# Third up product in wide multiplications over bank pairs, with GpSimd multiplying by the norm row

## The chip, the cores and the metric

The kernel runs on one core of a Trainium2 chip. Its time is the device time of one execution in microseconds (us); the number given for a kernel is the median over several runs. Beside it there is one profiled execution, from which all rows below come. The core has five engines that run side by side and wait for each other through semaphores: TensorE (PE, its weight loads PEld), VectorE (DVE), ScalarE (ACT), GpSimd (POOL) and SyncE (SP), which starts the transfers. TensorE writes to PSUM, which has 8 banks of 512 float32 for each of 128 partitions; all else lies in SBUF.

## The reference

Two blocks of a transformer run over one sequence of T = 256 tokens with 1024 features, all in float32. The first block has a short-convolution layer and a dilated-attention layer, each with a SwiGLU. The second ("hybrid") block has a gated mixture of attention and pooling, and then this feed-forward part, to which the change belongs:

```python
def causal_depthwise_conv(u, w, b):     # kernel width 3: token t sees t, t-1, t-2
def rmsnorm(x, g):
    y = xf * lax.rsqrt(jnp.mean(xf * xf, axis=-1, keepdims=True) + EPS)
    return (y * g).astype(x.dtype)
...
    h2 = rmsnorm(x, norm_ffn_g)
    up = causal_depthwise_conv(h2 @ w_up, conv_w, conv_b)
    gate, val = jnp.split(up, 2, axis=-1)
    return x + (jax.nn.silu(gate) * val) @ w_down
```

w_up is 1024 x 5632, w_down 2816 x 1024. The factor 1/rms of a token can be taken out of the product: h2 @ w_up is (x g) @ w_up, times one number per token, the "norm row".

## The kernel before

Float32 accuracy is made out of three products in a reduced format: each operand is split into a high part and a low rest, and high x high, high x low and low x high are summed in PSUM. ScalarE makes the high part of the weights (`w_hi`, line 1359) and VectorE the low rest (`w_lo = raw - w_hi`, line 1858). Activations are kept the same way, in `x_both`, where for each k the 256 tokens of `x_hi` stand beside the 256 of `x_lo` only by a stride, so that one multiplication of 512 columns can read both.

All weights stream through in chunks. A chunk of the third up product (`up2`, 22 chunks, written j = 0 to 3 within turns i, of which i = 1 to 4 are a hardware loop) is 1024 x 256: 8 blocks of k by 2 blocks of 128 output features. Even j is a gate chunk, odd j the value chunk for the same features; a unit is one pair. A chunk passes through these hands:

- SyncE loads it in two halves (line 583) into one of two raw buffers once VectorE is through with the raw chunk two before (`lo_ready`).
- ScalarE splits off the high part three chunks ahead of the one that it is treating, VectorE the low part two chunks ahead (`ahead(..., split, 3)` and `ahead(..., split, 2)`). Both are 2 instructions of 128x1024. There are four weight slots.
- TensorE waits for `lo_ready` and for the bank (`ready`), then runs `feature_major` (lines 667 to 686): for each of the 2 blocks and 8 k three multiplications of 256 columns, all into one bank, `s = (ph.n0 + j) % 4`. For `up2` this is bank 3, 0, 1, 2 for j = 0 to 3.
- VectorE multiplies the bank by the norm row (`rstd`, read again for both blocks through a stride of zero, `by_token`) into `scaled` (line 2053), and signals `emptied`. Then it does its weight splits.
- ScalarE makes the tap of the token itself with the bias, `gate = scaled * w2 + b` (line 1550, two instructions), and signals `conv_base`. For an even chunk it then makes the high part of the unit before (`last_high`, line 1538), for an odd one the silu of the gate (line 1558), and after that its weight split.
- VectorE adds the two earlier tokens (line 2063, four instructions of 128x255 or 128x254) and signals `taps_done`.
- GpSimd multiplies silu(gate) by value for a unit (`mid`, line 2497) and, when ScalarE has its high part, subtracts to get the low one (`a_lo`, line 2488). It does nothing else in this phase.

The first two chunks are treated apart (line 1169): their multiplications are interleaved with the last turning of x, and the norm row is only made in their course, through bank 7. After `up2` comes `down2`, 8 chunks of 5 or 6 k by 512 columns, whose first weights are split while the last up chunks are treated: these splits are of 128x1536 (or 1024).

The first block's up products (`up0`, `up1`) already use `gated_blocks` (lines 826 to 839). There the high weights are multiplied by both halves of `x_both` in one multiplication of 512 columns into a whole bank per block (left half high x high, right half high x low), and the low weights by `x_hi` in one of 256 into the left half. ScalarE copies the right halves out of the two banks, VectorE adds the left halves to them, and VectorE multiplies by the norm row.

Of the kernel before, what the change touches and what calls it, by code (L numbers as in the profile page):

```python
# [32 lines left out]
T = 256  # L33
# [64 lines left out]
def build(nc, a, out):  # L98
# [4 lines left out]
    with ctx:  # L103
# [218 lines left out]
        silu_done = sem("silu_done")  # L322
        conv_base = sem("conv_base")
        taps_done = sem("taps_done")
        gates_set = sem("gates_set")
        mid_ready = sem("mid_ready")
        mid_hi = sem("mid_hi")
# [88 lines left out]
        ROW_BANK = {0: 6, 1: 3, 2: 7, 3: 3, 4: 7, 5: 7}  # L416
        first_unit = {"up0": 0, "up1": 1}
        UNIT_TURN = 2
        NORM_OF = {"up0": 1, "up1": 3}

        def made(ph, u):
# [237 lines left out]
        def _(pe):  # L659
# [460 lines left out]
            def emit(ph):  # L1120
# [46 lines left out]
                elif name == "up2":  # L1167
                    def body(j, i):
                        if isinstance(i, int) and i == 0 and j < 2:
                            if j == 1:  # L1170
                                return
                            ready(ph, 0, 0)
                            feature_part(ph, 0, x_hi, x_lo, 5, 0, 3)
                            turn_x_pairs(5, 1)
                            feature_part(ph, 0, x_hi, x_lo, 5, 3, 4)
                            ready(ph, 1, 0)
                            feature_part(ph, 1, x_hi, x_lo, 5, 0, 4)
                            feature_part(ph, 0, x_hi, x_lo, 5, 4, KD).then_inc(product_done, 1)
                            row(5)
                            feature_part(ph, 1, x_hi, x_lo, 5, 4, KD).then_inc(product_done, 1)  # L1180
                            return
                        ready(ph, j, i)
                        feature_major(ph, j, x_hi, x_lo)
                    run(pe, ph, body, peel=1)
                elif name in ("pool_in", "gates_a"):
                    if name == "pool_in":
# [162 lines left out]
        def _(act):  # L1349
# [190 lines left out]
            def up_conv_body(ph):  # L1540

                def body(j, i):
                    first = isinstance(i, int) and i + j == 0
                    u = i * 2 + j // 2
                    if j % 2 == 0 and not first:
                        act.wait_ge(mid_ready, 4 + u)
                    wait_emptied(act, ph, j, i)
                    for m in range(2):
                        f = i * 4 + (j // 2 * 2 + j % 2 * KF + m)
                        ins = nc.scalar.activation(gate[:, j % 2, m, :], scaled[:, j % 2, m, :], ACT.Identity,  # L1550
                                                   bias=vec[:, ds(f + col["conv_b_2"], 1)],
                                                   scale=vec[:, ds(f + col["conv_w_2_2"], 1)])
                    ins.then_inc(conv_base, 1)
                    if j % 2 == 0 and not first:
                        last_high(ph, u - 1)
                    if j % 2 == 1:
                        act.wait_ge(taps_done, i * 4 + j)
                        nc.scalar.activation(flat2(gate[:, 0]), flat2(gate[:, 0]), ACT.Silu).then_inc(silu_done, 1)
                    ahead(ph, j, i, split, 3)
                return body  # L1560

            def softmax_exp(src, spans, c, at_):
# [283 lines left out]
        def _(dve):  # L1846
# [198 lines left out]
            def up_conv_body(ph):  # L2045

                def body(j, i):
                    first = isinstance(i, int) and i == 0 and j < 2
                    s = (ph.n0 + j) % 4
                    dve.wait_ge(product_done, ph.n(j, i) + 1)  # L2050
                    if not first:
                        dve.wait_ge(taps_done, i * 4 + (j - 1))
                    nc.vector.tensor_tensor(scaled[:, j % 2], ps[:, s, :].rearrange("p (m t) -> p m t", m=2),
                                            by_token(rstd), ALU.mult).then_inc(emptied[s], 1)
                    if not (first and j == 0):
                        ahead(ph, j, i, split, 2)
                    dve.wait_ge(conv_base, i * 4 + (j + 1))
                    wait_emptied(dve, ph, j, i)
                    for back in (1, 2):
                        for m in range(2):  # L2060
                            f = i * 4 + (j // 2 * 2 + j % 2 * KF + m + (2 - back) * 2 * KF)
                            o = gate[:, j % 2, m, back:T]
                            ins = nc.vector.scalar_tensor_tensor(
                                out=o, in0=scaled[:, j % 2, m, 0:T - back],
                                scalar=vec[:, ds(f + col["conv_w_2_01"], 1)], in1=o, op0=ALU.mult, op1=ALU.add)
                        if back == 1:
                            link(ins)
                    ins.then_inc(taps_done, 1)
                return body
# [411 lines left out]
        def _(pool):  # L2481
# [6 lines left out]
                nc.gpsimd.tensor_tensor(lo[:, ds(k0, 2), :], mid[:, half], hi[:, ds(k0, 2), :], ALU.subtract)\  # L2488
                    .then_inc(mid_split, 1)

            def last_unit(i, half):

                u = i * 2 + half
                pool.wait_ge(silu_done, u + 1)
                pool.wait_ge(taps_done, u * 2 + 2)
                pool.wait_ge(mid_split, u + unit0["up2"])
                nc.gpsimd.tensor_tensor(flat2(mid[:, 0]), flat2(gate[:, 0]), flat2(gate[:, 1]), ALU.mult)\
                    .then_inc(mid_ready, 1)
                hidden_low(a_hi, a_lo, u + unit0["up2"], u * 2, 0)

            def pool_windows():

# [12 lines left out]
            for ph, bi in order():  # L2515
                if ph is not None:
# [2 lines left out]
                        for i in range(4):  # L2519
                            hidden_low(a_hi, a_lo, i, 2 * i, i % 2)  # L2520
                    elif name == "up2":
                        last_unit(0, 0)
                        last_unit(0, 1)
                        with pool.Fori(1, 5) as i:
                            for half in range(2):
                                last_unit(i, half)
                        last_unit(5, 0)
                    elif name == "branches":
                        for j in range(4):
                            pool.wait_ge(mid_hi, unit0[name] + j + 1)  # L2530
                            nc.gpsimd.tensor_tensor(mix_lo[j // 2][:, j % 2 * 2:j % 2 * 2 + 2, :], mid[:, j % 2],
                                                    mix_hi[:, 2 * j:2 * j + 2, :], ALU.subtract).then_inc(mid_split, 1)
                    elif name == "pool_in":
                        pool.wait_ge(product_done, by_name["qkv2a"].n0)
                        nc.gpsimd.memset(u_pad[:, :, 0:16], 0.0).then_inc(zeroed, 1)
                        pool.wait_ge(hybrid_in, 5 * 16)
                        for l in range(2):
                            wait_emptied(pool, ph, l, 0)
                        pool_windows()
# [66 lines left out]
```

## Time and profile before

| | |
|---|---|
| median of 3 runs | 1084.68 us (1083.58 to 1085.16) |
| the profiled execution | 1083.43 us, its span 1081.4 us |
| PE busy | 1070.7 us, 99% |
| DVE busy | 804.5 us, 74% |
| ACT busy | 647.8 us, 60% |
| POOL busy | 54.5 us, 5% |
| granted TensorE clock | 1.00 |

Busy times are unions of instructions' spans on an engine. The timeline gives an instruction's start and its length; on TensorE, which is pipelined, the distance from one start to the next says what an instruction costs, not its length. VectorE's and ScalarE's instructions overlap their neighbours by some 0.1 us, so there, too, distances from start to start are the better measure of a sequence. An instruction's length includes the time in which it stands still after it has started.

### The profile page before, as it was taken

What the parts mean: (1) busy time and instruction counts of PE and PEld (TensorE: products, weight loads), DVE (VectorE), ACT (ScalarE), POOL (GpSimd) and SP (SyncE); (2) the same over time, 40 slices, a digit from 0 to 9 for tenths busy, and PEclk for the clock granted to TensorE, in tenths of its full rate; (3) what the DMA queues carried; (4) which work ended last, traced back from release to release, by engine and by line L of the source; (5) the groups of instructions that cost most, each with busy time, mean ns of one, the idle gap of its engine ahead of it and who ended that gap; (6) DMA issues with size and microseconds to landing.
All of it is one profiled execution on the core that took longest, in us unless ns stands there. A gap on an engine that the chain in (4) does not pass through costs nothing.

```text
span 1081.4 us, 19548 instructions
## 1 busy us (share of the span) xinstructions
PE 1070.7 (99%) x7436; PEld 970.6 (90%) x7436; DVE 804.5 (74%) x1217; ACT 647.8 (60%) x976; POOL 54.5 (5%) x47
## 2 busy tenths in 40 slices
PE   8999999999999999999999999999999999999998
PEld 8998888888899999888878888889999989999987
DVE  5976878775598778788578778636796778889960
ACT  6546746464588777777576465535465756556650
POOL 0100000000000000000000000000200111222300
PEclk9999999999999999999999999999999999999999
DMA  8555665777286766652256657753454664665660
GB/s 273 174 192 180 210 213 163 239 256 223 78 226 188 200 172 171 184 164 86 82 176 218 208 174 250 274 157 98 136 166 132 200 214 121 191 192 177 235 234 20
DMA packets 220557, 195.91 MB, mean 181 GB/s; under 512 B 10137, under 2 KB 196045, under 8 KB 220493
## 3 DMA queue, kind: packets, MB, share of 16 engines
q1 hardware_dynamic: 220137, 194.82, 57.8%
q8 instruction: 43, 0.70, 0.3%
q10 hardware_dynamic: 356, 0.22, 0.1%
q14 instruction: 21, 0.17, 0.0%
HBM read 191.85 MB, written 1.05 MB: 178 GB/s over the span
## 4 chain that ended last, share of the span: by engine, by line
PE 91%; DVE 3%; ACT 2%; SPq 1%; DMA 1%; issue 1%; DVEq 0%; ACTq 0%
PE ps L833 14%; PE ps L682 8%; PE ps L683 8%; PE ps L684 8%; PE ps L837 7%; PE ps L739 7%; PE ps L738 7%; PE ps L737 7%; PE ps L906 6%; PE ps L907 3%; PE ps L852 2%; PE ps L851 2%; PE ps L850 2%; DVE w_lo L1858 2%; ACT w_hi L1359 1%; PE ps L751 1%
## 5 line engine op out<-in xcount | busy, mean ns | idle before, releaser
L1858 DVE TENSOR_TENSOR w_lo<-raw,w_hi 128x1024 fp32r<-128x1024 f32 (+1 forms) x298 | 399.0, 1382 | 56.4 <-ACT w_hi L1359 55.5
L1359 ACT ACTIVATE w_hi<-raw 128x1024 fp32r<-128x1024 f32 (+1 forms) x298 | 331.3, 1156 | 119.1 <-PE ps L739 38.2
L682 PE MATMUL ps<-x_both,w_hi 128*128 128x256 f32 x656 | 186.8, 285 | 0.2 <-DVE w_lo L1858 0.2
L684 PE MATMUL ps<-x_both,w_lo 128*128 128x256 f32 x656 | 185.6, 283 | 0.0
L683 PE MATMUL ps<-x_both,w_hi 128*128 128x256 f32 x656 | 185.6, 283 | 0.0
L833 PE MATMUL ps<-x_both,w_hi 128*128 128x512 f32 x640 | 153.0, 391 | 0.0
L833 PEld LDWEIGHTS ps<-x_both,w_hi 128*128 128x128 f32 x640 | 117.6, 188 | 23.4 <-DVE w_lo L1858 0.7
L682 PEld LDWEIGHTS ps<-x_both,w_hi 128*128 128x128 f32 x656 | 125.8, 192 | 1.8 <-issue 1.3
L683 PEld LDWEIGHTS ps<-x_both,w_hi 128*128 128x128 f32 x656 | 125.9, 192 | 0.0
L684 PEld LDWEIGHTS ps<-x_both,w_lo 128*128 128x128 f32 x656 | 125.8, 192 | 0.0
L737 PE MATMUL ps<-w_hi,a_hi 128*128 128x512 f32 x296 | 115.7, 391 | 0.0
L738 PE MATMUL ps<-w_lo,a_hi 128*128 128x512 f32 x296 | 115.2, 389 | 0.0
L739 PE MATMUL ps<-w_hi,a_lo 128*128 128x512 f32 x296 | 115.2, 389 | 0.0
L837 PEld LDWEIGHTS ps<-x_both,w_lo 128*128 128x128 f32 x640 | 82.1, 191 | 3.1
L837 PE MATMUL ps<-x_both,w_lo 128*128 128x256 f32 x640 | 83.0, 283 | 0.0
L739 PEld LDWEIGHTS ps<-w_hi,a_lo 128*128 128x128 f32 x296 | 55.6, 188 | 11.6
L738 PEld LDWEIGHTS ps<-w_lo,a_hi 128*128 128x128 f32 x296 | 55.6, 188 | 11.2
L737 PEld LDWEIGHTS ps<-w_hi,a_hi 128*128 128x128 f32 x296 | 55.6, 188 | 11.2
L1496 ACT ACTIVATE gu<-ps 128x512 f32<-128x512 f32 x20 | 12.0, 599 | 88.5 <-PE ps L837 88.5
L1597 ACT ACTIVATE rot_x<-rot_s 32x512 f32<-32x512 f32 x84 | 52.9, 630 | 15.9 <-DVE rot_s L2114 15.1
L906 PE MATMUL ps<-m_both,w_hi 128*128 128x512 f32 x168 | 60.4, 402 | 0.3 <-DVE v_tok L2153 0.3
L906 PE MATMUL ps<-x_both,w_hi 128*128 128x512 f32 x168 | 60.1, 399 | 0.0
(260 smaller groups left out, 1793.2 us busy)
## 6 DMA issues: line engine op xcount, KB each, us to landing
raw<-in_ffn_w_gate_up SPq DMA_DIRECT2D x80, 512.0 KB, 5.3
raw<-in_w_up SPq DMA_DIRECT2D x44, 512.0 KB, 4.4
raw<-in_ffn_w_down SPq DMA_DIRECT2D x24, 768.0 KB, 6.3
raw<-in_conv_w_in SPq DMA_DIRECT2D x24, 512.0 KB, 5.0
raw<-in_w_q SPq DMA_DIRECT2D x48, 256.0 KB, 4.7
raw<-in_w_kv SPq DMA_DIRECT2D x48, 256.0 KB, 4.4
raw_v<-in_w_kv SPq DMA_DIRECT2D x48, 256.0 KB, 3.8
raw<-in_w_in SPq DMA_DIRECT2D x20, 512.0 KB, 4.7
```

Source lines behind the costliest of these rows:

```text
L682: nc.tensor.matmul(o, wh[:, k0 + k, c], hi[:, k, :], start=(k == 0), stop=False)
L683: nc.tensor.matmul(o, wh[:, k0 + k, c], low, start=False, stop=False)
L684: ins = nc.tensor.matmul(o, wl[:, k0 + k, c], hi[:, k, :], start=False, stop=(k == kt - 1))
L737: nc.tensor.matmul(o, high, wh[:, k, :], start=(first and k == ks[0]), **flags)
L738: nc.tensor.matmul(o, high, wl[:, k, :], start=False, **flags)
L739: ins = nc.tensor.matmul(o, low, wh[:, k, :], start=False, **flags)
L833: nc.tensor.matmul(o, wh[:, k, c], x_both[:, :, (k) * T:(k + 1) * T], start=(k == 0), stop=False, skip_group_check=True)
L837: ins = nc.tensor.matmul(o[:, 0, :], wl[:, k, c], x_hi[:, k, :], start=False, stop=(k == KD - 1), skip_group_check=True)
L906: nc.tensor.matmul(o, wh[:, k, c], x, start=(k == 0), stop=False, skip_group_check=True)
L1359: nc.scalar.activation(w_hi[:, s, a * ph.cols:b * ph.cols], src, ACT.Copy)\
L1597: ins = nc.scalar.activation(rot_x[f:f + 32, :, :], rot_s[o:o + 32, n, :, :], ACT.Copy)
L1858: nc.vector.tensor_tensor(w_lo[:, s, c], src, w_hi[:, s, c], ALU.subtract)\
```

## The change

From the third chunk of `up2` on, TensorE uses `gated_blocks` over the bank pair `CONV_BANK[j]` = 2, 0, 4, 6 for j = 0 to 3, with its one product_done per chunk. In front of the fourth chunk (i, j) = (0, 3), TensorE waits until VectorE has emptied the first. ScalarE, at the head of each such chunk, waits for the product and for the taps of two chunks before, copies the right halves of the pair to `scaled`, and does its weight split right behind the copy, no longer at the end. VectorE adds the left halves to the copy and signals `emptied`. GpSimd then multiplies `scaled` by the norm row in place and signals `conv_scaled`, for which ScalarE's and VectorE's tap instructions wait. GpSimd's earlier work is interleaved with it: product of the unit before, multiplication for the even chunk, low part of the unit before, multiplication for the odd chunk.

```diff
+        CONV_BANK = (2, 0, 4, 6)
...
                         ready(ph, j, i)
-                        feature_major(ph, j, x_hi, x_lo)
+                        if isinstance(i, int) and (i, j) == (0, 3):
+                            wait_emptied(pe, ph, 0, 0)
+                        gated_blocks(ph, j, (0, 1), CONV_BANK[j], 0).then_inc(product_done, 1)
...
+                    plain_ = isinstance(i, int) and i == 0 and j < 2
+                    if not plain_:
+                        act.wait_ge(product_done, ph.n(j, i) + 1)
+                        act.wait_ge(taps_done, i * 4 + (j - 1))
+                        nc.scalar.activation(scaled[:, j % 2], ps[:, CONV_BANK[j]:CONV_BANK[j] + 2, T:2 * T], ACT.Copy)\
+                            .then_inc(conv_low, 1)
+                        ahead(ph, j, i, split, 3)
                     if j % 2 == 0 and not first:
                         act.wait_ge(mid_ready, 4 + u)
-                    wait_emptied(act, ph, j, i)
+                    if plain_:
+                        wait_emptied(act, ph, j, i)
+                    else:
+                        act.wait_ge(conv_scaled, i * 4 + (j - 1))
...
-                    ahead(ph, j, i, split, 3)
+                    if plain_:
+                        ahead(ph, j, i, split, 3)
...
-                    dve.wait_ge(product_done, ph.n(j, i) + 1)
-                    if not first:
-                        dve.wait_ge(taps_done, i * 4 + (j - 1))
-                    nc.vector.tensor_tensor(scaled[:, j % 2], ps[:, s, :].rearrange("p (m t) -> p m t", m=2),
-                                            by_token(rstd), ALU.mult).then_inc(emptied[s], 1)
+                    if first:
+                        ...
+                    else:
+                        dve.wait_ge(conv_low, i * 4 + (j - 1))
+                        nc.vector.tensor_tensor(scaled[:, j % 2], ps[:, CONV_BANK[j]:CONV_BANK[j] + 2, 0:T], scaled[:, j % 2],
+                                                ALU.add).then_inc(emptied[s], 1)
                     if not (first and j == 0):
                         ahead(ph, j, i, split, 2)
                     dve.wait_ge(conv_base, i * 4 + (j + 1))
-                    wait_emptied(dve, ph, j, i)
+                    if first:
+                        wait_emptied(dve, ph, j, i)
+                    else:
+                        dve.wait_ge(conv_scaled, i * 4 + (j - 1))
...
+            def scale_chunk(i, j):
+
+                wait_emptied(pool, by_name["up2"], j, i)
+                nc.gpsimd.tensor_tensor(scaled[:, j % 2], scaled[:, j % 2], by_token(rstd), ALU.mult).then_inc(conv_scaled, 1)
...
+            def conv_unit(i, half):
+
+                u = i * 2 + half
+                last_product(u - 1)
+                scale_chunk(i, 2 * half)
+                last_low(u - 1)
+                scale_chunk(i, 2 * half + 1)
```

## Rows read from the trace of the kernel before

**Rows 1.** The page: busy us (share) and instructions; the chain by engine.
```profile
PE 1070.7 (99%) x7436; PEld 970.6 (90%) x7436; DVE 804.5 (74%) x1217; ACT 647.8 (60%) x976; POOL 54.5 (5%) x47
...
PE 91%; DVE 3%; ACT 2%; SPq 1%; DMA 1%; issue 1%; DVEq 0%; ACTq 0%
```

**Rows 2.** Windows: stretch, busy us of PE, PEld, DVE, ACT, POOL, clock, DMA.
```profile
5.00:10.00 5.00, 2.68 (x17) 1.98 (x17) 1.86 (x5) 2.46 (x5) 0.00 (x0) 1.00 1.00 337
904.00:1019.00 115.00, 115.00 (x958) 114.91 (x957) 104.23 (x141) 74.22 (x102) 28.47 (x20) 1.00 0.61 192
```

**Rows 3.** Timeline of PE, third up product's and down product's start: start us, us, what.
```profile
903.17 0.28 PE L682 MATMUL ps<-x_both,w_hi 128*128 128x256 f32 x1
...
1018.37 0.40 PE L737 MATMUL ps<-w_hi,a_hi 128*128 128x512 f32 x1
...
1018.60 0.40 PE L738 MATMUL ps<-w_lo,a_hi 128*128 128x512 f32 x1
```

**Rows 4.** Timeline of PE, the first block's first up product.
```profile
115.70 3.93 PE L833 MATMUL ps<-x_both,w_hi 128*128 128x512 f32 x16
119.46 2.08 PE L837 MATMUL ps<-x_both,w_lo 128*128 128x256 f32 x16
121.37 0.60 PE L823 MATMUL ps<-ident,mid_t 128*128 128x128 f32 x4
...
228.03 0.40 PE L737 MATMUL ps<-w_hi,a_hi 128*128 128x512 f32 x1
```

**Rows 5.** Timeline of DVE, one pair of chunks in the loop.
```profile
937.93 0.69 DVE L2053 TENSOR_TENSOR scaled<-ps,rstd 128x512 f32<-128x512 f32 x1
938.53 2.35 DVE L1858 TENSOR_TENSOR w_lo<-raw,w_hi 128x1024 fp32r<-128x1024 f32 x2
940.80 1.90 DVE L2063 SCALAR_TENSOR_TENSOR gate<-scaled,vec,gate 128x255 f32<-128x255 f32 x4
943.78 0.69 DVE L2053 TENSOR_TENSOR scaled<-ps,rstd 128x512 f32<-128x512 f32 x1 [1.08 <-PE ps L684]
946.65 2.94 DVE L2063 SCALAR_TENSOR_TENSOR gate<-scaled,vec,gate 128x255 f32<-128x255 f32 x4
```

**Rows 6.** Timeline of ACT: the same pair, and a copy in the first block.
```profile
938.79 1.10 ACT L1550 ACTIVATE gate<-scaled,vec 128x256 f32<-128x256 f32 x2 [2.19 <-DVE scaled L2053]
...
944.71 1.10 ACT L1550 ACTIVATE gate<-scaled,vec 128x256 f32<-128x256 f32 x2 [2.39 <-DVE scaled L2053]
945.71 0.61 ACT L1538 ACTIVATE a_hi<-mid 128x512 f32 x1
946.23 2.00 ACT L1359 ACTIVATE w_hi<-raw 128x1024 fp32r<-128x1024 f32 x2
...
172.65 0.60 ACT L1496 ACTIVATE gu<-ps 128x512 f32<-128x512 f32 x1 [5.06 <-PE ps L837]
```

**Rows 7.** Timeline of POOL: a unit in the loop, and a subtraction of the branches.
```profile
942.78 1.29 POOL L2497 TENSOR_TENSOR mid<-gate 128x512 f32<-128x512 f32 x1 [6.49 <-DVE gate L2063]
946.52 1.38 POOL L2488 TENSOR_TENSOR a_lo<-mid,a_hi 128x512 f32 x1 [2.45 <-ACT a_hi L1538]
...
856.03 1.55 POOL L2531 TENSOR_TENSOR mix_lo<-mid,mix_hi 128x512 fp32r<-128x512 f32 x1 [63.05 <-ACT mix_hi L1817]
```

**Rows 8.** Timelines of DVE and POOL where they meet; two undisturbed ones (945.52, 1024.74).
```profile
945.52 1.22 DVE L1858 TENSOR_TENSOR w_lo<-raw,w_hi 128x1024 fp32r<-128x1024 f32 x1
946.65 1.52 DVE L2063 SCALAR_TENSOR_TENSOR gate<-scaled,vec,gate 128x255 f32<-128x255 f32 x1
...
909.74 1.96 DVE L1858 TENSOR_TENSOR w_lo<-raw,w_hi 128x1024 fp32r<-128x1024 f32 x1
...
1015.40 2.59 POOL L2488 TENSOR_TENSOR a_lo<-mid,a_hi 128x512 f32 x1 [2.32 <-ACT a_hi L1538]
...
1024.74 0.48 DVE L2063 SCALAR_TENSOR_TENSOR gate<-scaled,vec,gate 128x254 f32<-128x254 f32 x1
...
1025.14 1.75 DVE L1858 TENSOR_TENSOR w_lo<-raw,w_hi 128x1536 fp32r<-128x1536 f32 x1
...
1026.80 2.32 DVE L1858 TENSOR_TENSOR w_lo<-raw,w_hi 128x1024 fp32r<-128x1024 f32 x1
...
1025.35 2.69 POOL L2497 TENSOR_TENSOR mid<-gate 128x512 f32<-128x512 f32 x1 [7.36 <-DVE gate L2063]
```

**Rows 9.** Timelines of DVE and POOL at the third chunk.
```profile
909.13 0.69 DVE L2053 TENSOR_TENSOR scaled<-ps,rstd 128x512 f32<-128x512 f32 x1
909.74 3.09 DVE L1858 TENSOR_TENSOR w_lo<-raw,w_hi 128x1024 fp32r<-128x1024 f32 x2
912.75 2.82 DVE L2063 SCALAR_TENSOR_TENSOR gate<-scaled,vec,gate 128x255 f32<-128x255 f32 x4
...
909.31 1.29 POOL L2497 TENSOR_TENSOR mid<-gate 128x512 f32<-128x512 f32 x1 [35.83 <-DVE gate L2063]
```

**Rows 10.** Timeline of ACT: the weight splits behind the second chunk.
```profile
908.18 2.00 ACT L1359 ACTIVATE w_hi<-raw 128x1024 fp32r<-128x1024 f32 x2
```

More of the change, by code:

```diff
@@ L324, in build @@
         taps_done = sem("taps_done")
+        conv_low, conv_scaled = sem("conv_low"), sem("conv_scaled")
         gates_set = sem("gates_set")
@@ L2049, in body @@
                     s = (ph.n0 + j) % 4
-                    dve.wait_ge(product_done, ph.n(j, i) + 1)
-                    if not first:
-                        dve.wait_ge(taps_done, i * 4 + (j - 1))
-                    nc.vector.tensor_tensor(scaled[:, j % 2], ps[:, s, :].rearrange("p (m t) -> p m t", m=2),
-                                            by_token(rstd), ALU.mult).then_inc(emptied[s], 1)
+                    if first:
+                        dve.wait_ge(product_done, ph.n(j, i) + 1)
+                        nc.vector.tensor_tensor(scaled[:, j % 2], ps[:, s, :].rearrange("p (m t) -> p m t", m=2),
+                                                by_token(rstd), ALU.mult).then_inc(emptied[s], 1)
+                    else:
+                        dve.wait_ge(conv_low, i * 4 + (j - 1))
+                        nc.vector.tensor_tensor(scaled[:, j % 2], ps[:, CONV_BANK[j]:CONV_BANK[j] + 2, 0:T], scaled[:, j % 2],
+                                                ALU.add).then_inc(emptied[s], 1)
                     if not (first and j == 0):
@@ L2489, in hidden_low, with last_product @@
                     .then_inc(mid_split, 1)
-            def last_unit(i, half):
-                u = i * 2 + half
+            def scale_chunk(i, j):
+                wait_emptied(pool, by_name["up2"], j, i)
+                nc.gpsimd.tensor_tensor(scaled[:, j % 2], scaled[:, j % 2], by_token(rstd), ALU.mult).then_inc(conv_scaled, 1)
+            def last_product(u):
                 pool.wait_ge(silu_done, u + 1)
@@ L2498, in last_unit, with last_low @@
                     .then_inc(mid_ready, 1)
+            def last_low(u):
                 hidden_low(a_hi, a_lo, u + unit0["up2"], u * 2, 0)
+            def conv_unit(i, half):
[4 more added lines that the diff above has]
+                scale_chunk(i, 2 * half + 1)
             def pool_windows():
@@ L2521, in _ @@
                     elif name == "up2":
-                        last_unit(0, 0)
-                        last_unit(0, 1)
+                        conv_unit(0, 1)
                         with pool.Fori(1, 5) as i:
                             for half in range(2):
-                                last_unit(i, half)
-                        last_unit(5, 0)
+                                conv_unit(i, half)
+                        conv_unit(5, 0)
+                        last_product(10)
+                        last_low(10)
                     elif name == "branches":
```

## Prediction

> **What bounds the kernel now.** I read the page first: the busy table, then the chain that ended last. TensorE is busy 99% of the span and 91% of the chain is its matmuls [rows 1], so a change pays only through TensorE's own time, and costs only if it makes TensorE wait. Next the windows of the stage that the diff touches (third chunk to last of the hybrid up product, about 904 to 1019 us): TensorE is busy all of 115.0 us, but VectorE is at 104.2 us, ScalarE 74.2, GpSimd 28.5 [rows 2]. VectorE has 9% spare there: it is the next bound. So I read its timeline in that stage [rows 5] together with GpSimd's [rows 7], because two engines that look far from full can still block each other.
>
> **TensorE's part.** Removed: 16 x 3 = 48 multiplications of 256 columns per chunk. The stage runs from 903.17 us to the first down matmul at 1018.37: 115.20 us for 20 chunks, 5.76 a chunk, 120 ns a matmul [rows 3]. Added: 16 of 512 and 16 of 256 columns, which is what the first block's up product already does: from 115.70 to 228.03 us, less 0.81 us from 121.37 to 122.18 for two other jobs of TensorE, is 111.52 us for 20 chunks, 5.58 a chunk [rows 4]. The merge saves 0.184 us a chunk, 3.7 us in all. Its bounds are these two rows; nothing else in TensorE's stream changes, and the new bank pairs give as many chunks of room as the old banks (four). The added wait of the fourth chunk is for a VectorE instruction that began at 900.95 us, some 7 us before that chunk starts; it is over, and costs nothing.
> By the Trainium skill ("TensorE: Matmul & The Clock Gate", section Back-to-back issue gap) a warm matmul costs its columns plus about 2.5 ns; merging two would then save 16 x 2.5 ns a chunk, an estimate of 0.8 us in all. The rows above show 120 ns for 256 columns and about 228 for 512 (3.76 us from 115.70 to 119.46 for 16, the first included), so the trace gives more to the merge than the page does.
>
> **What the chain behind it gains.** Per chunk before: VectorE's scale out of PSUM (0.69 us, next instruction 0.60 later), two weight splits (2.27 us from start to next start), four tap instructions (1.75, about 0.1 more inside the loop for register work), 4.7 in all; ScalarE: two gates 1.10, two splits 2.0, silu or high copy 0.62 [rows 5, 6]. The change adds a ScalarE copy of 128x512 out of PSUM (0.60, the same copy stands in the first block [rows 6]), swaps VectorE's scale for an add of the same shape (one operand in PSUM; I take 0.69), and adds a GpSimd multiplication of 128x512 per chunk, 20 of them. GpSimd's only like operation takes 1.29 us, its subtraction 1.38 [rows 7]. ScalarE gets to about 4.3 us a chunk and GpSimd to 2 x 1.29 + 1.29 + 1.38 = 5.3 a pair: both fit in 11.15. On the shares alone, the change is free.
>
> **What those shares hide.** Where a GpSimd operation overlaps a VectorE instruction whose two inputs are both in SBUF, one of them stands still. Three places show VectorE held [rows 8]: a tap takes 1.52 instead of 0.48 us when GpSimd's subtraction starts 0.13 us ahead of it (+1.04); the split of 1024 columns takes 1.96 instead of 1.22 when the product is in its last part (+0.74) and 2.32 when GpSimd was waiting (+1.10). GpSimd in turn takes 2.59 us (at 1015.40) and 2.69 (at 1025.35, in the split of 1.75 that began at 1025.14): it waits for that one instruction, goes in between, and holds the next. VectorE's scale, with one input in PSUM, is not held: 0.69 beside GpSimd's 1.29 [rows 9]. A price of 1.05 to 1.10 per meeting, then. GpSimd's new multiplication begins on the very signal after which VectorE starts its two splits, so all 20 meet.
> The Trainium skill ("SBUF — State Buffer", section Who interferes with whom) has this as a lock that is held for the whole instruction, the loser fully blocked, also for a VectorE instruction with two SBUF inputs. The trace agrees in kind, and shows 1.05 rather than the whole 1.29 to 1.39 as lost; by the page's whole duration 40 new or kept meetings would cost an estimated 9 us more than my sum.
>
> **The walk, pair of chunks by pair of chunks, when VectorE sets the pace.** Times from the start of VectorE's add.
> Even chunk: the add 0.61. GpSimd's product of the unit before runs until 1.47 (909.31 + 1.29 - 909.13), so the splits take 3.01 (909.74 to 912.75) [rows 9]. Meanwhile GpSimd's new multiplication waits; it gets in after the first split at 2.5, ends at about 3.7, and holds the second split 1.08: splits over at 0.61 + 3.01 + 1.08 = 4.7. ScalarE's gates run 3.7 to 4.85, taps start at 4.9, take 1.75, and meet GpSimd's subtraction (+1.05), as they do in the loop now. 7.7, with register work 7.85.
> Odd chunk: 0.61 + 2.27 + 1.08 = 3.96 for add and splits; multiplication over at 1.75 + 1.2 = 2.95, gates at 4.1, taps 4.15 to 5.9; 6.05 with register work.
> A pair: 13.9 us, 6.95 a chunk, against 11.52 now and 11.15 that TensorE would want. TensorE gets the weights of chunk n + 2 only from the splits of chunk n, so it falls to this pace.
>
> **The sum.** Chunk 2's slot begins later than now: ScalarE does its copy only after the splits that run 908.18 to 910.17 [rows 10], so the add starts at about 910.8 instead of 909.13; this slot is free of the product and takes 6.9. Chunk 3: 5.95, to 923.7. Eight pairs (chunks 4 to 19): 111.2, to 1034.9. In chunk 20 the splits are those of the down weights, 1.75 instead of 1.22 each, so they end at 1034.9 + 4.7 + 1.06 = 1040.7, and that is when the down product can start; now it starts at 1018.37. +22.3 us. Chunk 21's splits end at about 1048.7, as the first down chunk ends (8.2 us, 36 matmuls of 0.23 [rows 3]); from there VectorE has little to do per down chunk and catches up, so nothing more is lost and nothing given back. The slack that swallows the first losses (now a chunk's weights are ready some 2.9 us ahead: splits over 2.87 us after the add's start, 943.78 to 946.65 [rows 5], against 5.76) is in this, because I compare ends, not paces. The profiled execution took 1083.43 us with a span of 1081.4; 1083.43 + 22.3 = 1105.7. It lay 1.25 below the median of the runs, so I name 1106.
>
> **Bounds.** Below: no waiting of VectorE for gates at all, the pair 13.4 instead of 13.9: -5 us. If a multiplication with the broadcast norm row holds VectorE only as the product's last part did (0.74): 20 x 0.34 = -7 more. Above: broadcast operand as dear as GpSimd's slowest like operation (1.55 [rows 7]): +0.26 on hold and gates, +5; a hand-off of 0.2 us instead of the near zero I took at two places a chunk (ScalarE's gates start 0.17 to 0.24 after the scale [rows 5, 6]): +6. Its own range: 1094 to 1119.
>
> **Rivals.**
> A, faster: the new multiplication holds nothing, or only idle time. Then the chain after a product is copy 0.6, add 0.7, multiplication 1.3, gates 1.1, taps 1.86 = 5.6 plus hand-offs, next add due at 5.58 + 0.65: it fits, TensorE keeps its pace and 3.7 us are won: 1083.4 - 3.7 = 1079.7. For it: shares; GpSimd's product sits mostly in VectorE's idle time today. Against: that idle time is after the taps, and the new multiplication doesn't fall there. 8%.
> B, slower still: VectorE's two splits go back to back and GpSimd gets in only behind them. Odd chunk: multiplication 2.9 to 4.1, gates to 5.3, taps to 7.2; even chunk 9.0; a pair 16.3: 8 x 2.4 + 3 = 22 more, 1128. Against it: GpSimd's 2.69 us at 1025.35 ended before the second split did [rows 8]. 7%.
> C, in between: only a part of the meetings cost (VectorE at 12.0 to 12.6 a pair, so 8 x 1.9 to 8 x 1.3 us below the forecast, a little less in the first chunks): 1089 to 1095. For it: I know no case in which GpSimd reads a broadcast row. 9%.
> D: TensorE's gaps of 1.4 in 7 us drop its granted clock to the 1.2 GHz level; matmuls at twice the time are 11 us a chunk, over 1180. Against: with 2.68 of 5 us busy, at 5 to 10 us, the clock column says 1.00 [rows 2]. 2%.
>
> **How the numbers follow.** Forecast 74%, C 9, A 8, B 7, D 2. The range 1089 to 1128 holds the forecast's own, C, and B at its edge; what is left out is A, D and the tails. A difference under 0.2% (2.2 us) can't be told from none by such runs: faster 8%, within 1%, slower 91%.
>
> **What would show it.** In the windows of the stage: TensorE busy well below the stretch, VectorE near full. The weight splits' mean on VectorE from 1.24 to about 1.9 us; the new GpSimd line at about 2 us, with its wait inside; a chunk at 6.9 to 7.0 us by VectorE's adds; TensorE idle before the 512-column line, released by VectorE's weight split. Wrong if the splits stay at 1.22 us, or if chunks come at 5.58.

## The result and the profile after

The changed kernel takes 1107.88 us (median of 4 runs, 1106.04 to 1110.7), the kernel before 1084.92 us (4 runs): ratio 1.0212, 95% interval 1.0194 to 1.0230. Forecast were 1106 us and a slower kernel. The profiled execution took 1106.04 us with a span of 1104.3.

The page first: busy times by engine, and the chain that ended last, by engine.

```profile
PE 1071.6 (97%) x7116; PEld 954.6 (86%) x7116; DVE 830.7 (75%) x1217; ACT 662.0 (60%) x996; POOL 98.7 (9%) x67
...
PE 79%; DVE 7%; ACT 4%; POOL 4%; issue 3%; DMA 1%; SPq 1%; ACTq 0%; DVEq 0%; POOLq 0%
```

TensorE's busy time is nearly as before [rows 1]: 320 matmuls fewer, but as many columns. What tells is that its idle time in the span grew from 10.7 to 32.7 us, that its share of the chain fell from 91 to 79%, and that GpSimd is now in the chain with 4%. The window of the stage says the same; columns as in [rows 2].

```profile
904.00:1019.00 115.00, 97.56 (x539) 83.32 (x538) 106.66 (x116) 71.90 (x103) 57.48 (x32) 1.00 0.49 149
```

In the same 115 us TensorE is busy 97.6 us instead of 115.0, and VectorE 106.7 instead of 104.2. The stage itself, from TensorE's timeline: first wide matmul, one start in the middle, first down matmul.

```profile
902.66 3.82 PE L835 MATMUL ps<-x_both,w_hi 128*128 128x512 f32 x16
...
934.90 3.92 PE L835 MATMUL ps<-x_both,w_hi 128*128 128x512 f32 x16 [1.28 <-DVE w_lo L1873]
...
1041.13 0.50 PE L739 MATMUL ps<-w_hi,a_hi 128*128 128x512 f32 x1 [2.15 <-DVE w_lo L1873]
```

From 902.66 to 1041.13 us are 138.5, against 115.2 [rows 3]: +23.3, the whole of the loss (the medians differ by 23.0). In nearly every chunk TensorE waits for VectorE's weight split before the first 512-column matmul, 18 times and 19.9 us in all. One pair of chunks on VectorE, to be compared with [rows 5]:

```profile
922.87 0.68 DVE L2071 TENSOR_TENSOR scaled<-ps,scaled 128x512 f32<-128x512 f32 x1
923.47 4.26 DVE L1873 TENSOR_TENSOR w_lo<-raw,w_hi 128x1024 fp32r<-128x1024 f32 x2
928.17 2.72 DVE L2084 SCALAR_TENSOR_TENSOR gate<-scaled,vec,gate 128x255 f32<-128x255 f32 x4 [0.43 <-ACT gate L1564]
930.81 0.68 DVE L2071 TENSOR_TENSOR scaled<-ps,scaled 128x512 f32<-128x512 f32 x1
931.41 3.44 DVE L1873 TENSOR_TENSOR w_lo<-raw,w_hi 128x1024 fp32r<-128x1024 f32 x2
935.18 1.91 DVE L2084 SCALAR_TENSOR_TENSOR gate<-scaled,vec,gate 128x255 f32<-128x255 f32 x4 [0.33 <-ACT gate L1564]
937.00 0.68 DVE L2071 TENSOR_TENSOR scaled<-ps,scaled 128x512 f32<-128x512 f32 x1
```

The even chunk takes 7.94 us (922.87 to 930.81), the odd one 6.19, a pair 14.13 instead of 11.5. Two splits take 3.44 instead of 2.35 where GpSimd's new multiplication meets them, 4.26 where its product does too. GpSimd's side of it, to be compared with [rows 7] and [rows 9]:

```profile
923.13 1.29 POOL L2522 TENSOR_TENSOR mid<-gate 128x512 f32<-128x512 f32 x1 [3.13 <-DVE gate L2084]
924.38 2.28 POOL L2515 TENSOR_TENSOR scaled<-scaled,rstd 128x512 f32<-128x512 f32 x1
928.73 1.49 POOL L2509 TENSOR_TENSOR a_lo<-mid,a_hi 128x512 f32 x1 [2.07 <-ACT a_hi L1542]
931.57 2.20 POOL L2515 TENSOR_TENSOR scaled<-scaled,rstd 128x512 f32<-128x512 f32 x1 [1.35 <-DVE scaled L2071]
```

The multiplication stands behind VectorE's first split and then holds the second. All this is the forecast's walk. One thing on ScalarE's timeline is not: its weight split behind the copy waits for a transfer, 2.67 us here and 2.94 at the most, and the gates stand behind it.

```profile
935.47 0.58 ACT L1553 ACTIVATE scaled<-ps 128x512 f32<-128x512 f32 x1
936.42 1.06 ACT L1363 ACTIVATE w_hi<-raw 128x1024 fp32r<-128x1024 f32 x1 [0.37 <-DMA raw<-in_w_up]
940.15 1.06 ACT L1363 ACTIVATE w_hi<-raw 128x1024 fp32r<-128x1024 f32 x1 [2.67 <-DMA raw<-in_w_up]
941.12 1.08 ACT L1564 ACTIVATE gate<-scaled,vec 128x256 f32<-128x256 f32 x2
```

In the kernel before that split stood last in the chunk, and ScalarE waited for transfers of `w_up` nowhere in this stage. In 14 of the 20 chunks the gates then still wait for GpSimd's product, 18.3 us in all; in the others, as above, the late split is what they waited for. So a total as forecast is no proof of its parts. The experiments take the parts away one at a time.

### The profile page after: what moved, and what is told of

The parts are those of the page before. It is cut to its first block, busy times and chain, and to the rows that moved or that the text cites. A ratio compares the mean times of both kernels' runs of the same rounds, so it can differ in the third digit from the quotient of the medians.

```text
span 1104.3 us, 18956 instructions
## 1 busy us (share of the span) xinstructions
PE 1071.6 (97%) x7116; PEld 954.6 (86%) x7116; DVE 830.7 (75%) x1217; ACT 662.0 (60%) x996; POOL 98.7 (9%) x67
## 3 DMA queue, kind: packets, MB, share of 16 engines
HBM read 191.85 MB, written 1.05 MB: 175 GB/s over the span
## 4 chain that ended last, share of the span: by engine, by line
PE 79%; DVE 7%; ACT 4%; POOL 4%; issue 3%; DMA 1%; SPq 1%; ACTq 0%; DVEq 0%; POOLq 0%
PE ps L835 14%; PE ps L839 7%; PE ps L739 7%; PE ps L741 7%; PE ps L740 7%; PE ps L908 6%; PE ps L684 4%; PE ps L685 4%; PE ps L686 4%; DVE w_lo L1873 3%; PE ps L909 3%; POOL scaled L2515 2%; PE ps L854 2%; PE ps L852 2%; PE ps L853 2%
## 5 line engine op out<-in xcount | busy, mean ns | idle before, releaser
L1873 DVE TENSOR_TENSOR w_lo<-raw,w_hi 128x1024 fp32r<-128x1024 f32 (+1 forms) x298 | 426.3, 1474 | 56.4 <-ACT w_hi L1363 55.3
L835 PE MATMUL ps<-x_both,w_hi 128*128 128x512 f32 x960 | 231.5, 393 | 19.9 <-DVE w_lo L1873 19.9
L835 PEld LDWEIGHTS ps<-x_both,w_hi 128*128 128x128 f32 x960 | 176.1, 188 | 58.7 <-DVE w_lo L1873 16.6
L839 PEld LDWEIGHTS ps<-x_both,w_lo 128*128 128x128 f32 x960 | 123.1, 191 | 4.7
L839 PE MATMUL ps<-x_both,w_lo 128*128 128x256 f32 x960 | 124.5, 283 | 0.0
L740 PE MATMUL ps<-w_lo,a_hi 128*128 128x512 f32 x296 | 115.2, 389 | 0.0
L741 PE MATMUL ps<-w_hi,a_lo 128*128 128x512 f32 x296 | 115.2, 389 | 0.0
L684 PE MATMUL ps<-x_both,w_hi 128*128 128x256 f32 x336 | 96.3, 287 | 0.2 <-DVE w_lo L1873 0.2
L686 PE MATMUL ps<-x_both,w_lo 128*128 128x256 f32 x336 | 95.0, 283 | 0.0
L685 PE MATMUL ps<-x_both,w_hi 128*128 128x256 f32 x336 | 95.0, 283 | 0.0
L684 PEld LDWEIGHTS ps<-x_both,w_hi 128*128 128x128 f32 x336 | 64.4, 192 | 1.8 <-issue 1.3
L685 PEld LDWEIGHTS ps<-x_both,w_hi 128*128 128x128 f32 x336 | 64.4, 192 | 0.0
L686 PEld LDWEIGHTS ps<-x_both,w_lo 128*128 128x128 f32 x336 | 64.4, 192 | 0.0
L908 PE MATMUL ps<-x_both,w_hi 128*128 128x512 f32 x168 | 60.0, 398 | 0.0
```

What stands on the lines that cost most here:

```text
L684: nc.tensor.matmul(o, wh[:, k0 + k, c], hi[:, k, :], start=(k == 0), stop=False)
L685: nc.tensor.matmul(o, wh[:, k0 + k, c], low, start=False, stop=False)
L686: ins = nc.tensor.matmul(o, wl[:, k0 + k, c], hi[:, k, :], start=False, stop=(k == kt - 1))
L740: nc.tensor.matmul(o, high, wl[:, k, :], start=False, **flags)
L741: ins = nc.tensor.matmul(o, low, wh[:, k, :], start=False, **flags)
L835: nc.tensor.matmul(o, wh[:, k, c], x_both[:, :, (k) * T:(k + 1) * T], start=(k == 0), stop=False, skip_group_check=True)
```

## The experiments

Three rounds each unless said, beside runs of the kernel before on the same chip (medians 1084.7 to 1085.5). "Stage" is the time from the first matmul of the third chunk to the first down matmul in the run's profile; it is 115.2 in the kernel before and 138.5 in the changed one. Runs e2, e3, e4, f1, f2 and g2 leave the norm row out of the result.

| run | what differs from the changed kernel | median us | ratio to before, 95% | stage us |
|---|---|---|---|---|
| e1 | VectorE multiplies | 1105.49 | 1.0186 (1.0169 to 1.0203) | 135.7 |
| e2 | nobody multiplies | 1098.56 | 1.0127 (1.0110 to 1.0143) | 127.8 |
| e3 | GpSimd multiplies, nobody waits | 1104.62 | 1.0181 (1.0164 to 1.0198) | 134.6 |
| e4 | GpSimd hardly reads, all wait | 1106.81 | 1.0202 (1.0185 to 1.0219) | 136.5 |
| f1 | e2, split last again | 1081.90 | 0.9965 (0.9951 to 0.9979) | 112.3 |
| f2 | e3, split last again | 1102.01 | 1.0150 (1.0128 to 1.0171) | 132.4 |
| f3 | e1, split in halves | 1094.66 | 1.0087 (1.0070 to 1.0103) | 124.2 |
| f4 | kernel before, split early | 1099.15 | 1.0130 (1.0111 to 1.0150) | 127.2 |
| g1 | ScalarE's split in halves | 1106.28 | 1.0197 (1.0178 to 1.0216) | 137.2 |
| g2 | e4, split in halves | 1106.96 | 1.0210 (1.0193 to 1.0227) | 135.9 |
| m1 (5 rounds) | odd chunks wide, VectorE does both | 1083.91 | 0.9990 (0.9979 to 1.0000) | 114.0 |
| m2 (5 rounds) | m1, GpSimd subtracts | 1087.68 | 1.0022 (1.0012 to 1.0033) | 117.5 |

**e1: VectorE multiplies by the norm row.**

```diff
 # VectorE, behind its add
+wait_emptied(dve, ph, j, i)
+nc.vector.tensor_tensor(scaled[:, j % 2], scaled[:, j % 2], by_token(rstd), ALU.mult).then_inc(conv_scaled, 1)
 # GpSimd, conv_unit
-scale_chunk(i, 2 * half)
-scale_chunk(i, 2 * half + 1)
```

> The changed kernel with one thing moved: VectorE multiplies by the norm row itself, right behind its add, and GpSimd doesn't. Theory H (VectorE is the bound, and GpSimd's multiplication costs it 1.05 to 1.1 us per meeting): VectorE's own work is 0.6 + 0.6 + 2.27 + 1.86 = 5.3 a chunk, and per pair 1.05 for the subtraction and up to 0.74 for the product, so 11.7 to 12.5 a pair instead of 14.1: 1084 to 1091 us, though VectorE does more work than in the changed kernel. Rival L (what costs is the longer row of hands: ScalarE's copy ahead, the add behind it, the bank pairs, whoever multiplies): stays at 1100 or more. Rival R (VectorE is simply short of time, adding 0.6 of work a chunk makes it worse): above 1108.

Measured 1105.49 us, 14.5 us above the top of what theory H allowed: without any GpSimd multiplication the kernel is hardly faster. By the numbers rival L was right.

**e2: nobody multiplies.** As e1, without the multiplication; gates and taps wait for `emptied`.

> The changed kernel with the multiplication by the norm row left out altogether (taps read the unscaled sum). It shows the merge, the copy, the add and the bank pairs by themselves. Theory H: VectorE 9.5 of own work a pair plus 1.05 to 1.8 held is below 11.15, TensorE keeps 5.58 a chunk: 1083.4 - 3.7 = 1079.7, 1079 to 1082. Rival L: still above 1090.

Measured 1098.56, against 1079 to 1082 expected. Here VectorE isn't even full (95.2 us of 115 in the window 904 to 1019). Its timeline, and ScalarE's beside it, name what is:

```profile
922.35 3.17 DVE L1873 TENSOR_TENSOR w_lo<-raw,w_hi 128x1024 fp32r<-128x1024 f32 x2
927.06 2.71 DVE L2084 SCALAR_TENSOR_TENSOR gate<-scaled,vec,gate 128x255 f32<-128x255 f32 x4 [1.54 <-ACT gate L1564]
```

```profile
922.51 1.06 ACT L1363 ACTIVATE w_hi<-raw 128x1024 fp32r<-128x1024 f32 x1 [1.50 <-DMA raw<-in_w_up]
924.77 1.06 ACT L1363 ACTIVATE w_hi<-raw 128x1024 fp32r<-128x1024 f32 x1 [1.19 <-DMA raw<-in_w_up]
925.73 1.08 ACT L1564 ACTIVATE gate<-scaled,vec 128x256 f32<-128x256 f32 x2
```

VectorE is through with its splits at 925.5 and stands 1.54 us for the gates. The add is done since 922.4, but in ScalarE's queue the gates stand behind a split whose second half waits for its transfer until 924.77. That is a round: a raw buffer is freed by VectorE's split, the transfer takes some 4 us (median 4.1 from issue to landing in this run's stage, 4.4 in the kernel before), then ScalarE's split, gates, taps, and VectorE's next splits. I had costed the move of `ahead(..., split, 3)` only at the first chunk. I call this theory Q (queue), and the two parts of my walk H (holds) and W (the wait for GpSimd's result).

**e3: the holds without the wait.** GpSimd writes its product into a spare place, and gates and taps wait for `emptied`; only the reuse of its input waits for it.

```diff
 ...                                   # waits that guard the reuse of the buffers
-nc.gpsimd.tensor_tensor(scaled[:, j % 2], scaled[:, j % 2], by_token(rstd), ALU.mult).then_inc(conv_scaled, 1)
+nc.gpsimd.tensor_tensor(mid[:, 1], scaled[:, j % 2], by_token(rstd), ALU.mult).then_inc(conv_scaled, 1)
```

> GpSimd makes the same 20 multiplications at the same places, but into a spare place, and nobody waits for the result but the reuse of its input buffer; the taps read the unscaled sum (norm row left out). The hold stays, the wait for the result goes. Theory H: VectorE still loses 1.05 to 1.1 at each of 20 meetings, only its waits for the gates go: 13.2 to 13.5 a pair, 1098 to 1103. Rival W (what costs is the wait for GpSimd's result, 2.2 us, in the row of hands): back at TensorE's pace, 1080 to 1083.

1104.62: above the range of theory H, and with Q in it no proof of H.

**e4: the wait without the reading.**

```diff
 ...                                   # a wait that guards the order of the signals
-nc.gpsimd.tensor_tensor(scaled[:, j % 2], scaled[:, j % 2], by_token(rstd), ALU.mult).then_inc(conv_scaled, 1)
+nc.gpsimd.tensor_tensor(mid[:, 1, 0, 0:16], scaled[:, j % 2, 0, 0:16], rstd[:, 0:16], ALU.mult)
+nc.gpsimd.memset(spare[:], 0.0).then_inc(conv_scaled, 1)     # 128x1216
```

> The opposite: instead of multiplying, GpSimd does one multiplication of 16 columns and one memset of 128x1216, which reads nothing, together about 1.3 us, and the taps wait for it as for the product (norm row left out). The wait stays, the reading goes. Theory H: VectorE's splits aren't held; a slot is add 0.7, 1.3 to 1.4, gates 1.1, taps 1.86 = 5.0 to 5.1, under 5.58, plus the old holds: 1080 to 1084. Rival W: 1095 or more.

1106.81, expected 1080 to 1084: rival W's range. GpSimd's timeline says why the wait is longer than I took it for:

```profile
931.89 1.13 POOL L2518 TENSOR_TENSOR mid<-scaled,rstd 128x16 f32<-128x16 f32 x1 [1.36 <-DVE scaled L2072]
932.97 1.10 POOL L2519 MEMSET spare<- 128x1216 f32 x1
```

and VectorE's, beside it:

```profile
931.73 2.37 DVE L1874 TENSOR_TENSOR w_lo<-raw,w_hi 128x1024 fp32r<-128x1024 f32 x2
935.49 1.90 DVE L2085 SCALAR_TENSOR_TENSOR gate<-scaled,vec,gate 128x255 f32<-128x255 f32 x4 [1.39 <-ACT gate L1565]
```

16 columns take 1.13 us, since they too stand behind VectorE's first split. The result comes 1.1 + 1.1 us after the add, as late as the real multiplication (2.2). VectorE's two splits beside it take 2.37 us, so the memset holds nothing; VectorE idles 1.39 to 1.48 us a chunk for the gates instead of being held. So half of this wait is the same meeting seen from the other side: GpSimd's small reading stands still until the split is through. No run has GpSimd's result come early, 1.3 us after the add as the expectation took it, and such a short wait by itself stays untested.

**f1: e2 with ScalarE's split last again.**

```diff
 nc.scalar.activation(scaled[:, j % 2], ps[:, CONV_BANK[j]:CONV_BANK[j] + 2, T:2 * T], ACT.Copy).then_inc(conv_low, 1)
-ahead(ph, j, i, split, 3)
 ...                                   # gates, high copy or silu
-if plain_:
-    ahead(ph, j, i, split, 3)
+ahead(ph, j, i, split, 3)
```

> The run without any multiplication by the norm row (1098.6 us) with one thing put back: ScalarE's weight split again at the end of a chunk, behind gates and silu, not between its copy and the gates. New theory Q (in ScalarE's queue the gates stand behind a weight split whose raw data are still on their way: 43 us of waiting for transfers in that stage, and VectorE then waits for the gates): gone, since nothing that VectorE waits for in this slot stands behind the split; copy 0.6, add 0.7, gates 1.1, silu 0.5, split 1.95 = 4.9 us fit in 5.58: TensorE's pace, 1079 to 1082. Rival L (the wide form itself, the copy, the bank pairs): still 1095 to 1099.

1081.90 against 1085.50 for the kernel before: 3.6 us faster (2.3 to 5.3 by the interval). The queue order alone was worth 16.7 us (1098.56 to 1081.90), and the wide form with copy, add and bank pairs wins about the 3.7 us that the first step of the forecast gave it. Rival L is out.

**f2: e3 with the split last again.** It differs from f1 by 20 multiplications of GpSimd for which VectorE and ScalarE's gates don't wait (only the copy two chunks later does, as in e3).

> The run in which GpSimd multiplies into a spare place and nobody waits for the result (1104.6 us), again with ScalarE's weight split at the end. Norm row left out. The only difference to the run before it in this list is 20 multiplications of GpSimd. Theory H (a meeting costs VectorE 1.05 to 1.1): VectorE 13.2 to 13.5 a pair, some 17 to 20 us above the run without them: 1096 to 1102. If meetings cost nothing once the queue is right (Q alone): 1080 to 1083.

1102.01, 20.1 us above f1 and at the upper end of theory H's 1096 to 1102. VectorE, an even chunk of f1 and one of f2:

```profile
945.82 2.96 DVE L1871 TENSOR_TENSOR w_lo<-raw,w_hi 128x1024 fp32r<-128x1024 f32 x2
```

```profile
925.03 4.26 DVE L1873 TENSOR_TENSOR w_lo<-raw,w_hi 128x1024 fp32r<-128x1024 f32 x2
```

That is 1.3 us more; in odd chunks the two splits take 3.46 instead of 2.35, 1.1 more. Ten pairs would make 24 us, and the stage grew by 20.0: VectorE had some time to spare in f1 (108.5 us busy of 115).

**f3: e1 with the split in halves**, the first behind the copy, the second behind gates and silu.

```diff
-ahead(ph, j, i, split, 3)                                       # behind the copy
+ahead(ph, j, i, lambda *w: split(*w, parts=(0,)), 3)
...
-if plain_:
-    ahead(ph, j, i, split, 3)                                   # at the end
+ahead(ph, j, i, lambda *w: split(*w, parts=(0, 1) if plain_ else (1,)), 3)
```

> The run in which VectorE multiplies by the norm row (1105.5 us, correct output), with ScalarE's weight split in two: the first half behind the copy, the second behind gates and silu. Theory Q with H: gates wait for at most the first half; VectorE's own 5.3 a chunk and 1.05 to 1.8 held per pair: 11.7 to 12.5 a pair, 1084 to 1091 as I first expected of it. Without Q: still about 1105.

1094.66: 10.8 us faster than e1, as Q asks, but 4 us above the range in us. A pair takes 12.4 us on average of the stage, which is inside the 11.7 to 12.5 of the expectation; it was turned into a total wrongly, for ten pairs of 12.5 instead of 11.52 are 10 us and end at 1095, not at 1091. One part of the 12.4 is GpSimd's product, which now meets VectorE's multiplication at every even chunk (1.38 instead of 0.69):

```profile
924.42 1.38 DVE L2073 TENSOR_TENSOR scaled<-scaled,rstd 128x512 f32<-128x512 f32 x1
...
931.56 0.69 DVE L2073 TENSOR_TENSOR scaled<-scaled,rstd 128x512 f32<-128x512 f32 x1
```

**f4: the kernel before with nothing but the early split.**

```diff
+plain_ = isinstance(i, int) and i == 0 and j < 2
+if not plain_:
+    ahead(ph, j, i, split, 3)
 ...                                   # waits, gates, high copy or silu
-ahead(ph, j, i, split, 3)
+if plain_:
+    ahead(ph, j, i, split, 3)
```

> The kernel before, with nothing but ScalarE's weight split moved ahead of the gates from the third chunk on. No wide multiplication, no copy, no new work for GpSimd. Theory Q: the round split of VectorE, transfer of 4.6, second half of ScalarE's split 1.06, gates 1.1, taps 1.86, scale 0.6, splits 2.27, held 1.05 now and then, is 11.5 to 12.6 for two chunks against 11.52: 1086 to 1095, with ScalarE waiting for transfers 20 us or more and VectorE for gates. Rivals H and L: as before, 1084 to 1086.

1099.15: 13.7 us slower than the kernel before, more than the 1 to 10 that I gave it, from moving one call. No wide multiplication, no new work. VectorE and ScalarE:

```profile
924.84 3.12 DVE L1862 TENSOR_TENSOR w_lo<-raw,w_hi 128x1024 fp32r<-128x1024 f32 x2
931.08 2.95 DVE L2067 SCALAR_TENSOR_TENSOR gate<-scaled,vec,gate 128x255 f32<-128x255 f32 x4 [3.12 <-ACT gate L1553]
```

```profile
925.34 1.06 ACT L1359 ACTIVATE w_hi<-raw 128x1024 fp32r<-128x1024 f32 x1 [2.93 <-DMA raw<-in_w_up]
928.79 1.06 ACT L1359 ACTIVATE w_hi<-raw 128x1024 fp32r<-128x1024 f32 x1 [2.38 <-DMA raw<-in_w_up]
929.75 1.08 ACT L1553 ACTIVATE gate<-scaled,vec 128x256 f32<-128x256 f32 x2
```

**g1: the changed kernel with the split in halves** (f3's edit). **g2: e4 with the same.**

> The changed kernel, complete, with only ScalarE's weight split cut in two (first half behind the copy, second behind gates and silu), so that the gates no longer stand behind raw data that are late. Theory H + W (my walk on paper had no late transfers in it and gave 13.9 us a pair; measured 14.1): the holds and the wait for GpSimd's result set the pace by themselves, 1103 to 1107, almost nothing gained. If the queue (Q) is the larger part: 1097 or less.

> The run in which the taps wait for GpSimd though it hardly reads (one multiplication of 16 columns, one memset; norm row left out; 1106.8 us), with ScalarE's weight split cut in two, so that the gates stand behind no late raw data. Theory W (the wait for GpSimd's result is by itself enough: its small multiplication, too, stands 1.1 us behind VectorE's first split, so the result comes 2.3 us after the add, and add 0.6, 2.3, gates 1.1, taps 1.86, hand-offs and the old holds make 6.2 and 7.9 us slots): 1103 to 1107. If it was the queue (Q) that set this run's pace: 1090 or less.

g1 1106.28, g2 1106.96, both in the range of H + W and of W. With the queue mended nothing that is clear of noise is won (g1 against 1107.88, g2 against e4's 1106.81), because H and W, and W alone, keep the pace by themselves. In g1 the first half is over by 924.3, and the gates wait 2.9 us more for GpSimd; in g2 it is the same:

```profile
923.29 1.04 ACT L1363 ACTIVATE w_hi<-raw 128x1024 fp32r<-128x1024 f32 x1
927.22 1.10 ACT L1564 ACTIVATE gate<-scaled,vec 128x256 f32<-128x256 f32 x2 [2.89 <-POOL scaled L2514]
```

```profile
926.74 1.10 ACT L1565 ACTIVATE gate<-scaled,vec 128x256 f32<-128x256 f32 x2 [2.87 <-POOL spare L2518]
```

**m1 and m2: a version meant to beat both.** Only the odd chunks go wide, VectorE multiplies there, split in halves there and last elsewhere. In m1 VectorE also makes the low part of a unit (behind the even chunk's taps), in m2 GpSimd does as before.

```diff
-CONV_BANK = (2, 0, 4, 6)
+CONV_BANK = {0: 3, 1: 0, 2: 2, 3: 6}      # pairs at j = 1, 3; single banks at j = 0, 2
...
+if j % 2:
     gated_blocks(ph, j, (0, 1), CONV_BANK[j], 0).then_inc(product_done, 1)
+else:
+    feature_major(ph, j, x_hi, x_lo, bank=CONV_BANK[j])
...
+if j % 2 == 0 and not (first and j == 0):                       # VectorE, m1 only
+    dve.wait_ge(mid_hi, u + unit0[ph.name])
+    nc.vector.tensor_tensor(a_lo[:, k, :], mid[:, 0], a_hi[:, k, :], ALU.subtract).then_inc(mid_split, 1)
```

> A version meant to beat both: only the value chunks (every second one) in the wide form, VectorE multiplying by the norm row there, ScalarE's split cut in two in these chunks and at the end in the others, and VectorE subtracting for the low part of a unit instead of GpSimd. VectorE's own work is 5.35 + 5.45 = 10.8 us a pair, up to 0.7 held by the product; TensorE wants 5.76 + 5.58 = 11.34 instead of 11.52. All theories: TensorE stays full and 10 x 0.18 = 1.8 us are won against the kernel before, 1083 to 1084 where that one has 1085; if the product always meets a split, 11.5 and no gain.

> The same with GpSimd subtracting as in the kernel before. VectorE 10.2 of its own, 1.05 held by the subtraction, up to 0.7 by the product: 11.25 to 11.95 a pair against 11.34. Theory H: 1084 to 1088, up to 4 us above the run with VectorE's subtraction, although VectorE has 0.6 us less to do in a pair. Without holds: the same time as that run.

m1 1083.91, inside the expected 1083 to 1084, but the ratio is 0.9990 with 1.0000 at the interval's edge: no gain that can be told from none. A pair of m1 on VectorE, from one odd chunk's add to the next's:

```profile
927.68 0.68 DVE L2075 TENSOR_TENSOR scaled<-ps,scaled 128x512 f32<-128x512 f32 x1
...
933.69 3.15 DVE L1875 TENSOR_TENSOR w_lo<-raw,w_hi 128x1024 fp32r<-128x1024 f32 x2
936.76 1.89 DVE L2091 SCALAR_TENSOR_TENSOR gate<-scaled,vec,gate 128x255 f32<-128x255 f32 x4
938.57 0.68 DVE L2101 TENSOR_TENSOR a_lo<-mid,a_hi 128x512 f32 x1
939.17 0.68 DVE L2075 TENSOR_TENSOR scaled<-ps,scaled 128x512 f32<-128x512 f32 x1
```

11.49 us, and the product holds the even chunk's splits (3.15 for 2.35). That is the case for which the expectation named 11.5 and no gain. The even chunk's taps in m2, where GpSimd subtracts beside them:

```profile
926.12 2.99 DVE L2091 SCALAR_TENSOR_TENSOR gate<-scaled,vec,gate 128x255 f32<-128x255 f32 x4
```

m2 is 3.8 us slower than m1, 0.38 for each of 10 subtractions, though VectorE does less: the subtraction that costs VectorE 0.60 us (938.57 to 939.17) costs it 1.1 when GpSimd takes it over (taps of 2.99 for 1.89).

## Why the prediction was right, and where it wasn't

- **TensorE's 3.7 us.** Right: f1 shows 3.6. Chunks of f1 come at 5.57 us (904.93 to 910.50), forecast 5.58; its stage is only 2.9 us shorter than before, since the first down matmul still waits 0.84 for VectorE.
- **The price of a meeting, 1.05 to 1.10, and that all 20 meet.** Right: 20.1 us between f1 and f2; the changed kernel's splits take 1.1 more, and none of GpSimd's 20 multiplications is shorter than 2.20 us. The Trainium skill ("SBUF — State Buffer", section Who interferes with whom) lets a VectorE instruction with two SBUF inputs contend with a GpSimd instruction that reads SBUF, not with one that only writes it; the trace agrees, with e4's 16 columns standing still for a split and its memset beside 2.37 us of undisturbed splits. The price of a whole GpSimd instruction, by the prediction's estimate 9 us more, is not what the runs show.
- **The signs.** The splits' mean was to go from 1.24 to about 1.9 us in the stage, GpSimd's new line to about 2 (2.24 is its median), a chunk to 6.9 to 7.0 (138.5 for 20). VectorE was to be near full and is busy 106.7 of 115 us. Its group for 903 to 1045 us has 1930 ns:

```profile
L1873 DVE TENSOR_TENSOR w_lo<-raw,w_hi 128x1024 fp32r<-128x1024 f32 (+1 forms) x41 | 77.6, 1930 | 0.0
```

- **The walk.** 7.85 and 6.05 us forecast, 7.94 and 6.19 measured. The down product's start was forecast at 1040.7 and measured at 1041.13, though this stage began 0.5 us earlier (902.66 for 903.17): eight pairs took 112.3 us instead of 111.2 (VectorE's adds at 922.87 and 1035.18). Rival B (GpSimd only behind both splits) is refuted by the 2.2 to 2.3 us of its multiplication in the pairs, C by both chunks of a pair being held all through the stage.
- **A slip in the bounds.** The upper terms, +5 and +6, end at 1117 and not at the 1119 that stands there; two hand-offs of 0.2 us in 20 chunks would be 8. It changes nothing in the outcome.
- **What I missed.** "What the chain behind it gains" and the walk costed ScalarE's early split only in the first slot, and nowhere the late raw data that the gates now stand behind. It is worth 13.7 us in the kernel before (f4) and 16.7 in e2. That it costs next to nothing in the changed kernel (1107.88 against 1106.28 in g1) is luck, and for that reason the total didn't show it. Seven runs and the changed kernel are every combination of the three parts (W alone and W with Q by e4's stand-in for the product; without Q, the split is last in f1 and f2 and in halves in g1 and g2):

| parts in the kernel | run | stage us |
|---|---|---|
| none | f1 | 112.3 |
| Q | e2 | 127.8 |
| H | f2 | 132.4 |
| W | g2 | 135.9 |
| H and Q | e3 | 134.6 |
| W and Q | e4 | 136.5 |
| H and W | g1 | 137.2 |
| all three | changed | 138.5 |

Alone they cost 15.5, 20.0 and 23.6 us, which would add up to 59; together they cost 26.2. They lie beside each other on one round, so the slowest counts and the others add little: taking one away from all three gives back 1.3 (Q), 2.0 (H) or 3.9 us (W). Rival A was priced wrong for the same reason: without any hold of GpSimd's multiplication the kernel would still have been at 1098 or more (e2), not at 1079.7. Had the multiplication cost nothing, I would have forecast a gain and seen a loss of 13.
- **Rival D.** Not in the profiled execution: the granted clock is 1.00 in the stage, the 2.4 GHz level. But see the last section.

Not settled: a share of the 138.5 us for each of H, W and Q. The question has no single answer where each makes most of the loss alone. H and W also have one root, the meeting of GpSimd with VectorE's splits, and no run separates a wait for GpSimd from it. Not tried: a multiplication that sums both halves of `x_both` into the same columns, which would give the merge without VectorE's extra pass.

## What to carry to other kernels

When work moves to an engine that looks idle, ask which instructions of the full engine it stops, not what share it has left: here GpSimd's multiplication cost VectorE 1.1 us where VectorE's own would have cost 0.6. When a call moves up in a queue, list what stands behind it and what it itself waits for, a transfer above all; moving one split cost 13.7 us. And a total that comes out as forecast doesn't prove the mechanism; only the runs that took the parts away, one by one and together, showed three of them, each of which alone makes 15 to 24 of the 26 us.

## What the hardware showed unasked

After a gap TensorE can come back on the lower clock. In e2 it stood idle 1.83 us, and the next 16 matmuls took 5.53 us in place of 3.82; the granted clock of that window of 20 us was 0.91 (of 945.9 to 951.4 us 0.69, a mean of the two levels). The Trainium skill ("TensorE: Matmul & The Clock Gate", section Back-to-back issue gap) gives the gap between matmuls at both levels; by it 512 columns at 1.2 GHz would be about 427 ns, an estimate. The trace fits: from start to start these 16 take 336 ns each, between that and the 228 of the full clock.

```profile
940.00:960.00 20.00, 18.17 (x96) 15.64 (x95) 17.43 (x25) 13.52 (x21) 4.31 (x3) 0.91 0.48 147
...
945.92 5.53 PE L835 MATMUL ps<-x_both,w_hi 128*128 128x512 f32 x16 [1.83 <-DVE w_lo L1873]
...
953.19 3.82 PE L835 MATMUL ps<-x_both,w_hi 128*128 128x512 f32 x16
```

In e1 the 16 behind a gap of 3.20 us took 6.51, and the granted clock of 1032 to 1034 us was 0.50, the 1.2 GHz level:

```profile
1032.15 6.51 PE L835 MATMUL ps<-x_both,w_hi 128*128 128x512 f32 x16 [3.20 <-DVE w_lo L1873]
```

Other gaps as long as e2's passed without it (e1: 2.19 us before 964.13, the 16 matmuls took 3.96). It is rival D in small. The spread of the changed kernel's runs goes with the clock: the one with 1.000 took 1106.04, those with 0.997 to 0.998 took 1107.76, 1108.01 and 1110.7. But new gaps are not needed for that: of the 23 runs of the kernel before that stand beside m1, the 12 with clock 1.000 have a median of 1083.96 and the 11 below it 1085.63, with no idle TensorE in this stage. Those executions have no profile that would show where the clock fell.
